# Differential attention with its outputs kept by tokens

## The chip, the cores and the metric

The kernel runs on one core of one Trainium2 chip. The metric is the time on the device in microseconds (us): the median of the runs shown. The engines are TensorE (PE, with its weight loads PEld), VectorE (DVE), ScalarE (ACT), GpSimd (POOL) and the DMA queues.

## The reference

The program is a stack of four token mixers and six feed-forward blocks on 512 tokens of 1024 features, all in float32. Only one part is touched: the second half of the first mixer, differential attention with 8 heads. `q`, `k` and `v` are projections of the normed input; each head has two queries and two keys of 64 features and one value of 128.

```python
def block(start, q1b, q2b):
    mask = chunk_causal_mask(start, s)
    p1 = masked_softmax(einsum('bqhd,bkhd->bhqk', q1b, k1) * scale, mask)
    p2 = masked_softmax(einsum('bqhd,bkhd->bhqk', q2b, k2) * scale, mask)
    return einsum('bhqk,bkhe->bqhe', p1 - lam * p2, vf)

o = sweep_query_blocks(block, q[:, :, :, 0], q[:, :, :, 1])
o = rms_norm(o, subln) * (1.0 - lam_init)      # over a head's 128 features
```

The result, 1024 features, goes through an output projection. What matters here is the last line: each token's 128 outputs of a head are divided by the root of their mean square, and multiplied by a gain per feature.

## The kernel before, in words

Every engine has its program, written out in a fixed order, and semaphores order them among each other. `mm` (L316) issues one matmul; `pe_three` (L319 to L321) issues the three products of a float32 projection split into a high and a low part. Weights come as units of 128 x 1024 into a ring of six: DMA fills RAW, ACT rounds it (`hi_to`, L301), DVE takes the rest (`lo_to`, L307), and PE reports with `unit_done` when it has used it.

The stage is `ev_attn` (L1055). Its PE program interleaves several things. For head h, `scores(h, step)` makes the products of queries and keys, in three steps, into PSUM banks 2 to 5; DVE takes their maxima (`maxes`), ACT the exponentials with their sums (`exps`), and DVE subtracts the second map from the first (`combined`). `turn(h, g)` transposes the result in ten blocks of 128 x 128 into bank 6, in three groups, and ACT copies each group to PT (`turned`). `values(h)` multiplies by the values into bank 7: the stationary operand is V, so the output has features on partitions and tokens along the row; four products of 512, 384, 256 and 128 columns. Meanwhile PE projects the queries and keys of the head two further on (`pieces` into banks 0 and 1); ACT copies them (`query`), PE rotates them (`rot`), DVE finishes the rotation (`rope`). For h = 0 to 4 that is the loop over `early(h)`, some 20 us an iteration; behind it the order is written out by hand, with pieces of the output projection (`out_tile(m, k0, k1)`, which needs `yl` of heads below k1) put among the attention of heads 5 to 7.

The norm of a head, before: ACT copies the outputs from bank 7 to O (three buffers) and squares them to OSQ (`out`). PE sums the squares over the partitions with four products of one column (`squares`, L1171), DVE adds epsilon (`mean_square`), two heads' roots are taken at once (`roots`, eleven small instructions of 0.17 us), DVE writes them on the diagonals of four blocks (`diagonal`, L1532), and PE multiplies a matrix of ones by these, which puts each token's scale in bank 7 on all partitions (`scales`, L1177). DVE multiplies O by it and by the gain (`scaled`, L1540), ACT rounds the product to YH (`rounded`, L1394), DVE writes the rest to YL (`low`, L1544) and counts `yl`. Bank 7 is thus shared by values, squares and scales. A wait of one engine on another is a `wait_ge` on the semaphore, in the order of the program.

Of the kernel before, what the change touches and what calls it, by code (L numbers as in the profile page):

```python
# [1054 lines left out]
def ev_attn(nc, b):  # L1055
# [32 lines left out]
    DGA = sb("da_dg", [P, T], at=WORK2 + 13 * KB)  # L1088
# [3 lines left out]
    DG = [DGA, DGA, DGA, AB, DGA, AB, DGA, AB]  # L1092
    s = {n: sem("da_" + n) for n in """in v_ready qs_ready rot_ready rope_done angle_ready trig_ready lam_e
         scores max_ready p_ready comb tr pt_ready o_ready osq ssq ss_taken dg bc scaled yh yl""".split()}
# [12 lines left out]
    GROUPS = {4: (0, 1)}  # L1107
# [7 lines left out]
    def pe(pe, e):  # L1115
# [45 lines left out]
        def values(h):  # L1161
            pe.wait_ge(s["pt_ready"], 3 * h + 3)
            if h:
                pe.wait_ge(s["ss_taken"], h)
            if h in (3, 5, 7):
                pe.wait_ge(s["scaled"], {3: 2, 5: 4, 7: 5}[h])
            for j in range(TT):
                last = mm(ps[:, 7, j * P:T], V[:, j, tile(h)], PT[:, PTO[j]:PTO[j] + (4 - j) * P], j == 0, j == 3)
            last.then_inc(s["o_ready"], 1)

        def squares(h):  # L1171
            pe.wait_ge(s["osq"], 2 * h + 2)
            for j in range(TT):
                last = mm(ps[:, 7, j:j + 1], OSQ[:, tile(j)], ones[:, 0:1])
            last.then_inc(s["ssq"], 1)

        def scales(h, after):  # L1177

            pe.wait_ge(s["dg"], h + 1)
            pe.wait_ge(s["ss_taken"], after + 1)  # L1180
            if h:
                pe.wait_ge(s["scaled"], h)
            mm(ps[:, 7, :], ones[:], DG[h][:]).then_inc(s["bc"], 1)

# [22 lines left out]
        def early(h):  # L1207
# [10 lines left out]
            if h >= 2:  # L1218
                squares(h - 2)
# [4 lines left out]
            if h == 4:  # L1224
                scales(0, h - 2)
# [5 lines left out]
            if h == 4:  # L1231
                scales(1, h - 2)
# [15 lines left out]
        squares(3)  # L1248
# [15 lines left out]
        squares(4)  # L1264
# [4 lines left out]
        scales(2, 4)  # L1269
# [5 lines left out]
        scales(3, 4)  # L1275
# [11 lines left out]
        squares(5)  # L1287
# [12 lines left out]
        squares(6)  # L1300
# [3 lines left out]
        scales(4, 6)  # L1304
# [6 lines left out]
        squares(NH - 1)  # L1311
        out_tile(3, 2, 4)
        scales(5, NH - 1)
# [3 lines left out]
        scales(6, NH - 1)  # L1317
        out_tile(5, 3, 5)
        out_tile(0, 5, 6)
        scales(7, NH - 1)  # L1320
# [4 lines left out]
        pe.wait_ge(s["scaled"], NH)  # L1325
        out_whole(pe, no + 6, SCAN_BANK[6])

    def act(act, own, e):
# [56 lines left out]
        def out(h):  # L1385
            act.wait_ge(s["o_ready"], h + 1)
            if h >= 3:
                act.wait_ge(s["yl"], h - 2)
            A(O[:, h % 3, :], ps[:, 7, :], ACT.Copy).then_inc(s["osq"], 1)
            if h:  # L1390
                act.wait_ge(s["ssq"], h)
            A(OSQ[:], ps[:, 7, :], ACT.Square).then_inc(s["osq"], 1)

        def rounded(h):  # L1394
            act.wait_ge(s["scaled"], h + 1)
            A(YH[:, h, :], O[:, h % 3, :], ACT.Copy).then_inc(s["yh"], 1)

        for h in range(5):
            gq, gk = 4 + 2 * h, 5 + 2 * h
            if h >= 1:  # L1400
                exps(h - 1, 2)
            query(gq)
            hi_to(act, unit_of(e, gq) + 5)
            if h >= 1:
                turned(h - 1, 0)
            exps(h, 0)
            exps(h, 1)
            if h >= 1:
                turned(h - 1, 1)
                turned(h - 1, 2)  # L1410
            query(gk)
            hi_to(act, unit_of(e, gk) + 5)
            for a in GROUPS.get(h, ()):
                rounded(a)
            if h >= 1:
                out(h - 1)
# [40 lines left out]
    def dve(dve, own, e, finish, tail):  # L1457
# [65 lines left out]
        def mean_square(h):  # L1523
            dve.wait_ge(s["ssq"], h + 1)
            eps = EP[:, 4 * (h % 2):4 * (h % 2) + 4]
            own(v.scalar_tensor_tensor(SS[:, 4 * h:4 * h + 4], ps[:, 7, 0:4], 1.0 / P, eps, ALU.mult, ALU.add), "ss_taken")
# [5 lines left out]
        def diagonal(h):  # L1532
            if h in (1, 2):
                dve.wait_ge(s["bc"], h)
            elif h >= 4:
                dve.wait_ge(s["bc"], h - 1)
            own(v.tensor_tensor(DG[h][:].rearrange("p (j n) -> p j n", n=P), ident[:, None, :].to_broadcast([P, TT, P]),
                                RS[:, 4 * h:4 * h + 4][:, :, None].to_broadcast([P, TT, P]), ALU.mult), "dg")

        def scaled(h):  # L1540
            dve.wait_ge(s["bc"], h + 1)
            own(v.scalar_tensor_tensor(O[:, h % 3, :], O[:, h % 3, :], GAIN[:], ps[:, 7, :], ALU.mult, ALU.mult), "scaled")

        def low(h):  # L1544
            dve.wait_ge(s["yh"], h + 1)
            own(v.tensor_tensor(YL[:, h, :], O[:, h % 3, :], YH[:, h, :].bitcast(F32), ALU.subtract), "yl")

        for h in range(5):
# [10 lines left out]
            rope(gq)  # L1559
            if h == 4:  # L1560
                scaled(0)
                diagonal(1)
                scaled(1)
            combined(h, (0, 1))
            lo_to(dve, unit_of(e, gk) + 5)
            if h == 4:
                low(0)
                low(1)
            if h == 3:
                roots((0, 1))  # L1570
                diagonal(0)
# [15 lines left out]
        diagonal(2)  # L1587
# [4 lines left out]
        scaled(2)  # L1592
        diagonal(3)
        maxes(7, 0)
        scaled(3)
        maxes(7, 1)
        combined(6, (2,))
        low(2)
# [6 lines left out]
        roots((4, 5))  # L1605
        mean_square(6)
        diagonal(4)
        lo_to(dve, no + 6)
        scaled(4)
        low(4)  # L1610
        diagonal(5)
        mean_square(7)
        roots((6, 7))
        scaled(5)
        diagonal(6)
        low(5)
        diagonal(7)
        scaled(6)
        low(6)
        scaled(7)  # L1620
# [2279 lines left out]
```

## Time and profile before

| | us |
|---|---|
| median of 3 runs | 3405.75 |
| lowest, highest | 3405.64, 3407.36 |
| span of the profiled execution | 3408.6 |
| PE busy in it | 3352.6 |
| attention stage, within the window 100 to 275 us: PE busy | 171.5 of 175 |
| the same: DVE, ACT busy | 123.7, 82.5 |
| the same: granted clock | 1.00 |

The profile has no time of its own for that execution beside its span; the span is 2.85 us above the median of the runs. A timeline row is: start, duration, engine and line, operation, output and inputs, how many were merged, and in brackets how long the engine stood idle before it and for whom. Durations of PE contain the time that a result needs to leave the array, so what a group costs is read from one start to the next or from the chain. A float32 product of `mm` shows as two instructions. Rows of `mm` all have line 316 and are told apart by their tiles: `da_pt,da_v` is values, `ones,da_osq` squares, `da_dg,ones` or `da_ab,ones` scales, `da_k,da_q` scores, and `ident,da_p` on line 1157 a turn.

### The profile page before, as it was taken

The page shows a single profiled execution, that of the slowest core. Times are in us where ns is not written, and L with a number is a line of the kernel's source. Part 1 is how long each engine was busy: PE and PEld are TensorE (multiplying, and loading weights), DVE is VectorE, ACT ScalarE, POOL GpSimd, SP SyncE. Part 2 cuts the span into 40 slices and gives each one's busy share as a digit, 9 for nine tenths or more (in the row PEclk, how much of TensorE's full clock was granted, in tenths as well). Part 3 has the DMA queues.
Part 4 walks back from the last instruction along what each step waited for, and adds up shares of the span by engine and source line. Part 5 has one row for each costly group of instructions (what it writes and reads, how often), then busy time and mean ns, then how long its engine had stood idle before and what let it go on. Part 6 is the DMA issues. An engine that isn't in the chain of part 4 may idle for free.

```text
span 3408.6 us, 42717 instructions
## 1 busy us (share of the span) xinstructions
PE 3352.6 (98%) x17244; PEld 2790.3 (82%) x17244; DVE 1832.8 (54%) x2984; ACT 1311.8 (38%) x2216; POOL 17.2 (1%) x53
## 2 busy tenths in 40 slices
PE   8999999999999999999999999999999999999998
PEld 7768888888878888898888778888888888788887
DVE  5676884433886543354436357443454336664446
ACT  4453443222575322242224355322342226653333
POOL 0000000000100000000000000000000000000000
PEclk9999999999999999999999999999999999999999
DMA  3103213223301222322232211322322232023244
GB/s 131 62 25 108 69 63 109 95 100 100 102 21 56 93 99 98 106 93 99 96 103 94 87 38 66 106 95 100 104 93 94 98 105 77 32 81 105 97 144 167
DMA packets 92568, 307.81 MB, mean 90 GB/s; under 512 B 16014, under 2 KB 17684, under 8 KB 92372
## 3 DMA queue, kind: packets, MB, share of 16 engines
q1 hardware_dynamic: 89528, 301.31, 26.4%
q10 hardware_dynamic: 2844, 3.77, 0.3%
q8 instruction: 137, 2.24, 0.3%
q14 instruction: 59, 0.48, 0.0%
HBM read 302.95 MB, written 2.10 MB: 89 GB/s over the span
## 4 chain that ended last, share of the span: by engine, by line
PE 90%; DVE 6%; ACT 3%; issue 1%; DMA 0%; SPq 0%; DVEq 0%; ACTq 0%
PE ps L319 25%; PE ps L321 25%; PE ps L320 25%; PE ps L316 14%; DVE WL L307 1%; ACT WH L301 1%; DVE R L709 1%; PE ps L3103 0%; DVE XL L884 0%; DVE XT L875 0%; DMA RAW<-units 0%; DVE XT L878 0%; ACT XH L646 0%; ACT R L644 0%; DVE S L722 0%
## 5 line engine op out<-in xcount | busy, mean ns | idle before, releaser
L319 PE MATMUL ps<-XH,WH 128*128 128x512 f32 (+1 forms) x3200 | 1188.0, 371 | 19.1 <-DVE XL L884 12.7
L321 PE MATMUL ps<-XH,WL 128*128 128x512 f32 (+1 forms) x3200 | 1171.0, 366 | 0.0
L320 PE MATMUL ps<-XL,WH 128*128 128x512 f32 (+1 forms) x3200 | 1170.4, 366 | 0.0
L307 DVE TENSOR_TENSOR WL<-RAW,WH 128x1024 fp32r<-128x1024 f32 x567 | 686.3, 1224 | 312.6 <-ACT WH L301 308.6
L319 PEld LDWEIGHTS ps<-XH,WH 128*128 128x128 f32 x3200 | 606.5, 190 | 125.6 <-DVE XL L884 11.4
L321 PEld LDWEIGHTS ps<-XH,WL 128*128 128x128 f32 x3200 | 606.4, 190 | 96.6
L320 PEld LDWEIGHTS ps<-XL,WH 128*128 128x128 f32 x3200 | 607.0, 190 | 95.9 <-issue 1.9
L301 ACT ACTIVATE WH<-RAW 128x1024 fp32r<-128x1024 f32 x567 | 587.3, 1050 | 150.3 <-DMA RAW<-units 91.4
L319 PE MATMUL ps<-HH,WH 128*128 128x512 f32 (+1 forms) x990 | 362.7, 366 | 0.0
L320 PE MATMUL ps<-HL,WH 128*128 128x512 f32 (+1 forms) x990 | 361.8, 365 | 0.0
L321 PE MATMUL ps<-HH,WL 128*128 128x512 f32 (+1 forms) x990 | 361.7, 365 | 0.0
L596 ACT ACTIVATE HH<-HV 128x512 fp32r<-128x512 f32 x132 | 83.4, 632 | 564.3 <-DVE HV L788 564.3
L788 DVE SCALAR_TENSOR_TENSOR HV<-SG,ps 128x512 f32<-128x512 f32 x132 | 90.7, 687 | 294.7 <-PE ps L321 294.3
L785 DVE SCALAR_TENSOR_TENSOR SG<-TH,ps 128x512 f32<-128x512 f32 x132 | 90.7, 687 | 290.2 <-ACT TH L593 290.0
L503 ACT ACTIVATE SQ<-R 128x512 f32<-128x512 f32 (+1 forms) x89 | 48.9, 550 | 483.9 <-DVE R L709 408.0
L709 DVE SCALAR_TENSOR_TENSOR R<-R,ps 128x512 f32<-128x512 f32 (+1 forms) x86 | 51.5, 599 | 336.6 <-PE ps L321 335.8
L593 ACT ACTIVATE TH<-ps 128x512 f32<-128x512 f32 x132 | 78.7, 596 | 360.6 <-PE ps L321 360.6
L319 PEld LDWEIGHTS ps<-HH,WH 128*128 128x128 f32 x990 | 186.7, 189 | 30.5
L321 PEld LDWEIGHTS ps<-HH,WL 128*128 128x128 f32 x990 | 186.7, 189 | 30.1
L320 PEld LDWEIGHTS ps<-HL,WH 128*128 128x128 f32 x990 | 186.7, 189 | 30.0
L790 DVE TENSOR_TENSOR HL<-HV,HH 128x512 fp32r<-128x512 f32 x132 | 91.4, 693 | 101.4 <-ACT HH L596 101.4
L646 ACT ACTIVATE XH<-XT,VEC 128x256 fp32r<-128x256 f32 x144 | 78.9, 550 | 32.8 <-DVE XT L875 32.7
(603 smaller groups left out, 3258.8 us busy)
## 6 DMA issues: line engine op xcount, KB each, us to landing
RAW<-units SPq DMA_DIRECT2D x567, 512.0 KB, 3.3
XIN<-in_x ACTq DMA_DIRECT2D x2, 1024.0 KB, 6.3
out<-YT SPq DMA_DIRECT2D x8, 256.0 KB, 3.2
mb_pairf<-constants ACTq DMA_DIRECT2D x1, 512.0 KB
GB<-in_ln_g SPq DMA_DIRECT2D x1, 512.0 KB
GB<-in_ln_b SPq DMA_DIRECT2D x1, 512.0 KB
da_pi<-in_positions ACTq DMA_DIRECT2D x1, 256.0 KB, 3.0
wa_dist<-constants ACTq DMA_DIRECT2D x1, 192.0 KB, 2.3
```

What stands on the lines that cost most here:

```text
L301: nc.scalar.activation(WH[:, u % RING, :], RAW[:, u % RING, :], ACT.Copy).then_inc(S["wh_ready"], 1)
L307: nc.vector.tensor_tensor(WL[:, u % RING, :], RAW[:, u % RING, :], WH[:, u % RING, :].bitcast(F32), ALU.subtract)\
L316: return nc.tensor.matmul(out, lhsT, rhs, start=start, stop=stop, **kw)
L319: nc.tensor.matmul(out, wh, xh, start=start, stop=False)
L320: nc.tensor.matmul(out, wh, xl, start=False, stop=False)
L321: return nc.tensor.matmul(out, wl, xh, start=False, stop=stop)
L596: nc.scalar.activation(HH[:, j, :], HV[:, j % 2, :], ACT.Copy).then_inc(S["ffn_act"], 1)
L646: nc.scalar.activation(XH[:, k, hs], XT[:, t % 4, :], ACT.Identity, scale=g, bias=b).then_inc(S["xh_ready"], 1)
L709: own(v.scalar_tensor_tensor(rk, rk, alpha, src, ALU.mult, ALU.add), "r_ready")
L785: own(v.scalar_tensor_tensor(SG[:, j % 2, :], TH[:, j % 2, :], 1.0, ps[:, b, :], ALU.add, ALU.mult))
L788: own(v.scalar_tensor_tensor(HV[:, j % 2, :], SG[:, j % 2, :], e["half"], ps[:, b + 1, :], ALU.mult, ALU.mult), "ffn_dve")
L790: own(v.tensor_tensor(HL[:, j, :], HV[:, j % 2, :], HH[:, j, :].bitcast(F32), ALU.subtract), "ffn_dve")
```

## The change

`values(h)` swaps its operands: the transposed map is stationary and V moves, in ten products of 128 columns, so the output in bank 7 has tokens on partitions. The sum over a head's features is then along the row: ACT squares with an accumulator, one instruction for each of four token tiles, straight to SS. `squares`, `diagonal` and `scales` are gone. DVE multiplies O by the roots row by row (`scaled`), PE transposes the product back in four blocks into bank 7 or, for heads 4 and 6, bank 3 (`back`), ACT rounds it from there with the gain as its scale, and DVE writes the rest, again from PSUM. The semaphores change with it: `values` waits for `ssq` instead of `ss_taken`, and for heads 3 and 5 for `yl` of 2 and 4; `back` waits for `scaled`, for `ssq` and for an earlier `yl`. The orders of DVE and ACT around them change as shown (context cut).

```diff
@@ -1085,13 +1085,12 @@
     PT = sb("da_pt", [P, 1280], at=WORK2 + 8 * KB)
-    DGA = sb("da_dg", [P, T], at=WORK2 + 13 * KB)
     AB = sb("da_ab", [P, T], at=WORK2 + 16 * KB)
...
-    DG = [DGA, DGA, DGA, AB, DGA, AB, DGA, AB]
+    BACK = (7, 7, 7, 7, 3, 7, 3, 7)
     s = {n: sem("da_" + n) for n in """in v_ready qs_ready rot_ready rope_done angle_ready trig_ready lam_e
-         scores max_ready p_ready comb tr pt_ready o_ready osq ssq ss_taken dg bc scaled yh yl""".split()}
+         scores max_ready p_ready comb tr pt_ready o_ready ssq scaled back yh yl""".split()}
     MX, NM, L, RC, N2 = sm[:, 0:8], sm[:, 8:24], sm[:, 24:40], sm[:, 40:48], sm[:, 48:52]
...
@@ -1104,7 +1103,6 @@
     PTO = (0, 512, 1024, 896)
-    GROUPS = {4: (0, 1)}
...
@@ -1161,26 +1159,24 @@
             if h:
-                pe.wait_ge(s["ss_taken"], h)
-            if h in (3, 5, 7):
-                pe.wait_ge(s["scaled"], {3: 2, 5: 4, 7: 5}[h])
-            for j in range(TT):
-                last = mm(ps[:, 7, j * P:T], V[:, j, tile(h)], PT[:, PTO[j]:PTO[j] + (4 - j) * P], j == 0, j == 3)
+                pe.wait_ge(s["ssq"], h)
+            if h in (3, 5):
+                pe.wait_ge(s["yl"], {3: 2, 5: 4}[h])
+            for i in range(TT):
+                for j in range(i + 1):
+                    last = mm(ps[:, 7, tile(i)], PT[:, PTO[j] + (i - j) * P:PTO[j] + (i - j + 1) * P], V[:, j, tile(h)], j == 0, j == i)
             last.then_inc(s["o_ready"], 1)
-        def squares(h):
-            pe.wait_ge(s["osq"], 2 * h + 2)
-            for j in range(TT):
-                last = mm(ps[:, 7, j:j + 1], OSQ[:, tile(j)], ones[:, 0:1])
-            last.then_inc(s["ssq"], 1)
-
-        def scales(h, after):
-
-            pe.wait_ge(s["dg"], h + 1)
-            pe.wait_ge(s["ss_taken"], after + 1)
-            if h:
-                pe.wait_ge(s["scaled"], h)
-            mm(ps[:, 7, :], ones[:], DG[h][:]).then_inc(s["bc"], 1)
+        def back(h, after):
+
+            pe.wait_ge(s["scaled"], h + 1)
+            if BACK[h] == 7:
+                pe.wait_ge(s["ssq"], after + 1)
+            if BACK.index(BACK[h]) < h:
+                pe.wait_ge(s["yl"], h if h < 4 else h - 1)
+            for i in range(TT):
+                last = nc.tensor.transpose(ps[:, BACK[h], tile(i)], O[:, h % 3, tile(i)], ident[:])
+            last.then_inc(s["back"], 1)
...
@@ -1215,21 +1211,19 @@
                 turn(h - 1, 0)
-            if h >= 2:
-                squares(h - 2)
             if h:
...
             if h == 4:
-                scales(0, h - 2)
+                back(0, h - 2)
             if h >= 1:
...
             if h == 4:
-                scales(1, h - 2)
+                back(1, h - 2)
             pieces(n2 + 2 * h + 1, ps[:, 1, :], XH, XL, 6, KD)
...
@@ -1245,7 +1239,6 @@
         pieces(n2 + 11, ps[:, 1, :], XH, XL, 0, 1)
-        squares(3)
         pieces(n2 + 11, ps[:, 1, :], XH, XL, 1, 3)
...
@@ -1261,18 +1254,17 @@
         scores(6, 2)
-        squares(4)
         turn(5, 1)
...
         out_tile(0, 0, 2)
-        scales(2, 4)
+        back(2, 4)
         scores(7, 0)
...
         scores(7, 1)
-        scales(3, 4)
+        back(3, 4)
         out_tile(1, 1, 2)
...
@@ -1284,7 +1276,6 @@
         out_tile(2, 1, 2)
-        squares(5)
         turn(6, 2)
...
@@ -1297,32 +1288,29 @@
         turn(7, 1)
-        squares(6)
         out_tile(3, 1, 2)
...
         turn(7, 2)
-        scales(4, 6)
+        back(4, 6)
         out_tile(4, 2, 3)
...
         out_tile(4, 3, 4)
-        squares(NH - 1)
+        back(5, NH - 1)
         out_tile(3, 2, 4)
-        scales(5, NH - 1)
         out_tile(4, 4, 5)
...
         out_tile(3, 4, 5)
-        scales(6, NH - 1)
+        back(6, NH - 1)
         out_tile(5, 3, 5)
         out_tile(0, 5, 6)
-        scales(7, NH - 1)
+        back(7, NH - 1)
         for m in range(1, 6):
...
             out_tile(m, 6, KD)
-        pe.wait_ge(s["scaled"], NH)
         out_whole(pe, no + 6, SCAN_BANK[6])
...
@@ -1385,15 +1373,17 @@
             if h >= 3:
-                act.wait_ge(s["yl"], h - 2)
-            A(O[:, h % 3, :], ps[:, 7, :], ACT.Copy).then_inc(s["osq"], 1)
+                act.wait_ge(s["back"], h - 2)
+            A(O[:, h % 3, :], ps[:, 7, :], ACT.Copy)
             if h:
                 act.wait_ge(s["ssq"], h)
-            A(OSQ[:], ps[:, 7, :], ACT.Square).then_inc(s["osq"], 1)
+            for i in range(TT):
+                last = A(OSQ[:, tile(i)], ps[:, 7, tile(i)], ACT.Square, accum_out=SS[:, 4 * h + i:4 * h + i + 1])
+            last.then_inc(s["ssq"], 1)
         def rounded(h):
-            act.wait_ge(s["scaled"], h + 1)
-            A(YH[:, h, :], O[:, h % 3, :], ACT.Copy).then_inc(s["yh"], 1)
+            act.wait_ge(s["back"], h + 1)
+            A(YH[:, h, :], ps[:, BACK[h], :], ACT.Copy, scale=GAIN[:]).then_inc(s["yh"], 1)
...
@@ -1405,13 +1395,15 @@
             exps(h, 1)
+            if h == 4:
+                rounded(0)
             if h >= 1:
...
                 turned(h - 1, 2)
+            if h == 4:
+                rounded(1)
             query(gk)
             hi_to(act, unit_of(e, gk) + 5)
-            for a in GROUPS.get(h, ()):
-                rounded(a)
             if h >= 1:
...
@@ -1523,27 +1515,19 @@
             eps = EP[:, 4 * (h % 2):4 * (h % 2) + 4]
-            own(v.scalar_tensor_tensor(SS[:, 4 * h:4 * h + 4], ps[:, 7, 0:4], 1.0 / P, eps, ALU.mult, ALU.add), "ss_taken")
+            own(v.scalar_tensor_tensor(SS[:, 4 * h:4 * h + 4], SS[:, 4 * h:4 * h + 4], 1.0 / P, eps, ALU.mult, ALU.add))
...
-        def diagonal(h):
-            if h in (1, 2):
-                dve.wait_ge(s["bc"], h)
-            elif h >= 4:
-                dve.wait_ge(s["bc"], h - 1)
-            own(v.tensor_tensor(DG[h][:].rearrange("p (j n) -> p j n", n=P), ident[:, None, :].to_broadcast([P, TT, P]),
-                                RS[:, 4 * h:4 * h + 4][:, :, None].to_broadcast([P, TT, P]), ALU.mult), "dg")
-
         def scaled(h):
-            dve.wait_ge(s["bc"], h + 1)
-            own(v.scalar_tensor_tensor(O[:, h % 3, :], O[:, h % 3, :], GAIN[:], ps[:, 7, :], ALU.mult, ALU.mult), "scaled")
+            o = O[:, h % 3, :].rearrange("p (j n) -> p j n", n=P)
+            own(v.tensor_tensor(o, o, RS[:, 4 * h:4 * h + 4][:, :, None].to_broadcast([P, TT, P]), ALU.mult), "scaled")
...
             dve.wait_ge(s["yh"], h + 1)
-            own(v.tensor_tensor(YL[:, h, :], O[:, h % 3, :], YH[:, h, :].bitcast(F32), ALU.subtract), "yl")
+            own(v.scalar_tensor_tensor(YL[:, h, :], ps[:, BACK[h], :], GAIN[:], YH[:, h, :].bitcast(F32), ALU.mult, ALU.subtract), "yl")
...
@@ -1557,18 +1541,16 @@
             rope(gq)
+            combined(h, (0, 1))
             if h == 4:
-                scaled(0)
-                diagonal(1)
-                scaled(1)
-            combined(h, (0, 1))
+                low(0)
             lo_to(dve, unit_of(e, gk) + 5)
             if h == 4:
-                low(0)
                 low(1)
...
                 roots((0, 1))
-                diagonal(0)
+                scaled(0)
+                scaled(1)
...
@@ -1584,18 +1566,16 @@
         maxes(6, 1)
-        diagonal(2)
+        scaled(2)
         mean_square(4)
...
         rope(15)
-        scaled(2)
-        diagonal(3)
+        scaled(3)
         maxes(7, 0)
-        scaled(3)
+        low(2)
         maxes(7, 1)
         combined(6, (2,))
-        low(2)
         low(3)
...
@@ -1603,21 +1583,17 @@
         roots((4, 5))
+        scaled(4)
         mean_square(6)
-        diagonal(4)
+        scaled(5)
         lo_to(dve, no + 6)
-        scaled(4)
         low(4)
-        diagonal(5)
         mean_square(7)
         roots((6, 7))
-        scaled(5)
-        diagonal(6)
+        scaled(6)
+        scaled(7)
         low(5)
-        diagonal(7)
-        scaled(6)
         low(6)
-        scaled(7)
         low(7)
...
```

## Rows read from the trace of the kernel before

**Rows 1.** The page: busy time of each engine; the chain that ended last, by engine.
```profile
PE 3352.6 (98%) x17244; PEld 2790.3 (82%) x17244; DVE 1832.8 (54%) x2984; ACT 1311.8 (38%) x2216; POOL 17.2 (1%) x53
...
PE 90%; DVE 6%; ACT 3%; issue 1%; DMA 0%; SPq 0%; DVEq 0%; ACTq 0%
```

**Rows 2.** Chain of waits, 110 to 275 us: start us, us on the chain, what.
```profile
241.01 0.44 PE ps L1157 x4
...
248.25 2.39 PE ps L316 x8
...
254.08 0.79 PE ps L316 x8
254.87 0.35 PE ps L319
255.21 0.23 PE ps L320
...
256.38 0.86 PE ps L316 x2
```

**Rows 3.** Timeline of PE in the stage behind: start us, us, instructions [idle before].
```profile
322.45 1.05 PE L316 MATMUL ps<-mb_bc 128*128 128x128 f32 x8
323.33 0.49 PE L1696 MATMUL ps<-ident,mb_bc 128*128 128x128 f32 x3
```

**Rows 4.** Timeline of PE in the attention stage.
```profile
165.07 0.38 PE L1157 MATMUL ps<-ident,da_p 128*128 128x128 f32 x2
...
189.57 2.42 PE L316 MATMUL ps<-da_pt,da_v 128*128 128x512 f32 x8
...
216.94 1.05 PE L316 MATMUL ps<-ones,da_osq 128*128 128x1 f32 x8 [0.99 <-ACT da_osq L1392]
...
223.35 1.13 PE L316 MATMUL ps<-da_k,da_q 64*128 64x512 f32 x4 [1.75 <-DVE da_k L1480]
...
228.84 2.39 PE L316 MATMUL ps<-da_pt,da_v 128*128 128x512 f32 x8 [0.30 <-DVE da_o L1542]
...
248.25 2.39 PE L316 MATMUL ps<-da_pt,da_v 128*128 128x512 f32 x8 [0.23 <-DVE da_o L1542]
```

**Rows 5.** Groups of instructions by shape, 100 to 275 us.
```profile
L316 PEld LDWEIGHTS ps<-da_pt,da_v 128*128 128x128 f32 x64 | 11.6, 189 | 8.4 <-issue 5.2
```

**Rows 6.** Timeline of ACT in the attention stage.
```profile
123.58 0.37 ACT L1375 ACTIVATE da_p<-ps,da_small 128x128 f32<-128x128 f32 x1
...
123.92 0.38 ACT L1375 ACTIVATE da_p<-ps,da_small 128x128 f32<-128x128 f32 x1
...
163.89 0.60 ACT L1383 ACTIVATE da_pt<-ps 128x512 f32<-128x512 f32 x1
...
189.50 1.05 ACT L301 ACTIVATE WH<-RAW 128x1024 fp32r<-128x1024 f32 x1
...
215.81 0.59 ACT L1389 ACTIVATE da_o<-ps 128x512 f32<-128x512 f32 x1
...
216.77 0.59 ACT L1375 ACTIVATE da_p<-ps,da_small 128x384 f32<-128x384 f32 x1
...
235.05 0.60 ACT L1383 ACTIVATE da_pt<-ps 128x512 f32<-128x512 f32 x1 [0.95 <-PE ps L1157]
```

**Rows 7.** Timeline of DVE in the attention stage.
```profile
184.95 0.75 DVE L1542 SCALAR_TENSOR_TENSOR da_o<-da_o,da_gain,ps 128x512 f32<-128x512 f32 x1
...
188.50 0.17 DVE L1511 RECIPROCAL da_small<-da_small 128x3 f32<-128x3 f32 x1
...
190.66 1.23 DVE L307 TENSOR_TENSOR WL<-RAW,WH 128x1024 fp32r<-128x1024 f32 x1
...
219.23 0.18 DVE L1511 RECIPROCAL da_small<-da_small 128x3 f32<-128x3 f32 x1
```

**Rows 8.** Timeline of PE near 496 us, in a later stage.
```profile
495.77 0.39 PE L319 MATMUL ps<-XH,WH 128*128 128x256 f32 x1 [2.64 <-DVE XL L887]
```

**Rows 9.** Windows: us, busy per engine, granted clock (PEclk), DMA share, GB/s.
```profile
496.00:500.00 4.00, 4.00 (x21) 3.82 (x21) 3.63 (x8) 2.37 (x4) 0.00 (x0) 0.59 0.02 4
```

## The prediction

> **What bounds the kernel now.** I read the page first: TensorE (PE) is busy 98% of the span, DVE 54%, ACT 38%, and PE carries 90% of the chain that ended last [rows 1]. So work taken off PE counts in full wherever PE doesn't then wait, and a new wait of PE counts in full as well; DVE or ACT time counts only through such a wait. The PE timeline of the attention stage then gives the order of work, and four places where PE does wait: 0.99 us ahead of the squares of head 4, 1.75 ahead of the first scores of head 7, 0.30 and 0.23 ahead of the values of heads 5 and 7 [rows 4]. All that is edited lies between 127 and 265 us.
>
> **PE's work, per head.** The chain prices a PE group by what it adds to the path [rows 2]. Squares: eight pieces 0.79 us, and the matmul behind them takes 0.35 instead of 0.23, so 0.91. The broadcast of scales (two passes over 512 columns): 0.86. Both go. Four transposes come: the same form costs 0.44. Values: now 8 instructions (each product takes two passes), 2560 columns in all, 2.39 us of path; after, 20 instructions of 128 columns, the same columns. The trace has that form: 8 of 128x128 take 322.45 to 323.33, 0.11 each, so 20 take 2.20 [rows 3], and with the 0.12 that the next matmul loses 2.32. From -0.07 to a weight load that stops overlapping (20 by 189 ns, 3.8 us, +1.4 [rows 5]) I take no difference, by the row of the same form. PE is thus rid of 0.91 + 0.86 - 0.44 = 1.33 per head, 10.6 in all, and 0.99 + 0.30 + 0.23 of waits ahead of squares 4 and values 5 and 7 could go: 12.1 us if nothing else came late.
>
> The Trainium skill, "TensorE: Matmul & The Clock Gate", section LDWEIGHTS, puts a load of 128 columns at 128/1.2 = 107 ns whatever the rows. Added to the pass instead of hidden, twelve more loads would be 1.3 us a head and 10 us in all by that figure; the 0.11 per load and matmul together says that they overlap.
>
> **ACT and DVE.** ACT's one square of 512 (copy and square 215.81 to 216.77, 0.48 each) becomes four of 128 with an accumulator read each; exps of that width with their read come every 0.34 (123.58 to 123.92) [rows 6]. So 1.36, 0.9 more per head, between the output copy and what ACT does next. Bounds: 0.3 apiece if the missing bias pointer saves a little, 0.6 apiece if the 0.37 of the one and its read did not overlap with the next. DVE loses the diagonals (0.69) and writes the same 0.69 for the row scaling; `low` reads PSUM, 0.75 like the multiplication at 184.95 [rows 7]. mean_square no longer waits for PE. None of this matters except where a wait of PE hangs on it, so I walk PE's waits; times are those of before, shifts are noted.
>
> **Heads 2 and 3 of the loop (130 to 170 us): -0.5 each, not -0.9.** With squares gone PE reaches the last turn 0.91 sooner, 164.16 instead of 165.07. It needs ACT's copy of the turn before, 163.89 + 0.60 = 164.49, which hangs on exps that no edit moves. So it starts at 164.55 [rows 4, 6]: 0.52 gained, 0.4 turned into a wait. Twice: -1.05.
>
> **Head 4 (170 to 192 us): +3.3.** Three edits meet. (1) `back(1)` writes bank 7, so it waits for `low(0)`, and DVE does that behind rope and combined. Rope ended at 184.95 and PE's rotation that it waited for comes 0.9 sooner, of which some 0.6 is felt: 184.3. Combined with its upkeep took 188.50 to 190.66: 186.45. low(0) 0.75: 187.2. PE's turn ahead of it ends near 185.3, a stall of about 1.9; the broadcast it replaces began at 186.48 and cost twice as much, so PE leaves 0.2 later than before. (2) `values(3)` now waits for two `yl`, and `low(1)` sits on DVE behind lo_to, which waits for ACT's rounding of a weight, which ACT does behind query, which waits for PE to end the projection just before. Before: ACT rounds at 189.50, DVE's split starts at 190.66. With +0.2 the split starts at 190.85, is left 1.15 later, low(1) 192.0 to 192.75, values at 192.9 instead of 189.57 [rows 4, 6, 7]. PE has only scores(4,2) to do meanwhile: a stall of 3.1. Queued behind it are rot(13) and the next projection; ACT and DVE behind them wait for PE and lie inside the shift. This is the largest term. Sum so far +2.25.
>
> **Heads 5 to 7.** squares(3) gives -0.91. squares(4) and its wait of 0.99 vanish, but scores(7,0) waits for rope(15), the end of a DVE run that waits for exps(6,1). ACT's output copy goes from 215.81 to 214.90, squares end 0.49 + 1.36 later, 216.75, where exps(6,1) used to start: no gain. DVE's combined goes from 219.23 to 218.85, since it had followed a max that waited for PE. scores(7,0) goes from 223.35 to 222.97. So of 0.91 + 0.91 + 0.99 + 0.42 only 0.4 arrives; PE idles from 218.2, some 4.7 us. Then low(2) needs rounded(2), behind PE's turn(5,2): 225.4; low(2) ends 226.4; back(3) at 226.55, about even with the broadcast at 226.7. values(5) needs low(3): maxes(7,1) end with their scaling at 228.1, combined (a max's scaling, five small ones and a product, about 1.25) at 229.35, low(3) 230.1, values at 230.25 instead of 228.84: +1.4, a stall of 2.5. Then squares(5) gives 0.91 but ACT's 0.9 longer output delays its copy of turn(6,1) from 235.05 to 236.5, so the next turn goes from +1.4 to +0.8 only. squares(6) -0.91, broadcast 4 -0.42, wait ahead of values(7) -0.23: -0.75. Last, squares(7) and three exchanges: -0.91 - 3 x 0.42, so -2.9 at the end; low(6) and low(7) are needed 4 us after they are done. With +2.25: -0.65 us, where PE's own work fell by 10.6.
>
> **The clock.** Ahead of 495.77 PE was idle for 2.64 us, and the next 4 us had a granted clock of 0.59: 4 x 0.41 = 1.64 us lost, the lower of the two levels (1.2 against 2.4 GHz) for most of it [rows 8, 9]. Four new stalls (1.9, 3.1, 4.7, 2.5 us) can each call it; the idle 1.75 ahead of the scores of head 7 did not (the stage had full clock throughout). Behind values(3) PE works without a wait and would pay in full. I take one such fall: +1.65. The Trainium skill ("TensorE: Matmul & The Clock Gate", Part 1) says "the default state is throttled, and activity releases the throttle"; the row above agrees.
>
> Sum: -0.65 + 1.65 = +1.0 on the profiled span, 3408.6 to 3409.6. That execution's span is 2.85 above the median of the runs, 3405.75; the difference carries over, so 3406.8.
>
> **Rivals.** A. *The stalls are not there*, because the lows or ACT come earlier than I walk: the 12.1 us above, 3393.7. For: DVE is half idle. Against: the order of each engine's work is fixed, and low(1) stands behind a weight that waits for PE. Halfway, with the values(3) stall gone only: 3403. B. *No fall of the clock*: -0.65, 3405.1. C. *A fall behind each of the four stalls*: -0.65 + 4 x 1.64 = +5.9, 3411.7; from one more stall of 1 us on it is measurably slower. D. *Weight loads bound the values*: 20 x 0.189 = 3.8 instead of 2.39, +1.4 a head and +11 in all, 3405.75 - 0.65 + 11 = 3416, slower; it decides from 0.17 us per instruction (1.0 more a head). For: da_pt's loads show 189 ns. Against: 0.11 for the pair.
>
> **Chances.** One or two falls, 3405.5 to 3409: 0.50. B 0.20. Halfway 0.10. A 0.08. C 0.08. D 0.04. What can be told from no change here is 0.2%, 6.8 us. Faster than that: A and a little of halfway, 0.10. Slower: D and half of C, 0.08. Within: 0.82. The range 3400 to 3411 leaves out A, D and most of C.
>
> **What would show it.** Waits of PE: on DVE `da_yl` ahead of values(3), about 3 us, and of values(5), about 2.5; on ACT `da_pt` ahead of the last turn of heads 2 and 3, 0.4 each; on DVE rope ahead of scores(7,0), over 4. Values at 0.11 per instruction; four squares within 1.4 us; a granted clock under 1.00 between 190 and 235 us. PE's busy time should fall by about 9 and its idle rise as much. I am wrong if PE passes values(3) without a wait, or if values take over 2.6 us.

## Result and profile after

The changed kernel takes 3413.15 us (median of 20 runs, 3406.88 to 3416.84). The kernel before, run beside it, takes 3407.66 (20 runs, 3404.12 to 3411.68; the three runs known ahead had 3405.75). The ratio is 1.0013, interval 1.0007 to 1.0019: 4.4 us slower, 2.4 to 6.5. (The two medians lie 5.5 us apart, the means of the same runs, 3412.41 and 3407.95, 4.5.) The prediction was 3406.8, so a slowdown of 1.0, and a range that ended at 3411: too low, and the range missed. The profiled execution of the changed kernel took 3413.99, its span 3412.0.

The page of the kernel after, busy time and chain by engine, beside [rows 1]:

```profile
PE 3346.2 (98%) x17292; PEld 2792.6 (82%) x17292; DVE 1827.3 (54%) x2976; ACT 1315.1 (39%) x2272; POOL 17.6 (1%) x53
...
PE 89%; DVE 7%; ACT 3%; issue 1%; DMA 0%; DVEq 0%; ACTq 0%
```

PE has 6.4 us less busy time and the kernel is longer, so PE must stand idle where it did not before. The timeline of PE between 127 and 255 us says where (start us, us, what, idle before it and for whom):

```profile
127.59 2.50 PE L316 MATMUL ps<-da_v,da_pt 128*128 128x128 f32 x20
129.92 1.02 PE L316 MATMUL ps<-da_qs,da_perm 128*128 128x512 f32 x2
...
164.22 0.44 PE L1155 MATMUL ps<-ident,da_p 128*128 128x128 f32 x2
...
184.35 0.44 PE L1155 MATMUL ps<-ident,da_p 128*128 128x128 f32 x2 [0.23 <-ACT da_pt L1371]
...
186.49 0.63 PE L1178 MATMUL ps<-ident,da_o 128*128 128x128 f32 x4 [1.70 <-DVE da_yl L1530]
...
192.22 4.10 PE L316 MATMUL ps<-da_v,da_pt 128*128 128x128 f32 x20 [3.05 <-DVE da_yl L1530]
196.16 1.02 PE L316 MATMUL ps<-da_qs,da_perm 128*128 128x512 f32 x2
...
226.88 2.08 PE L316 MATMUL ps<-da_k,da_q 64*128 64x512 f32 x4 [4.18 <-DVE da_k L1472]
...
235.63 3.31 PE L316 MATMUL ps<-da_v,da_pt 128*128 128x128 f32 x20 [2.48 <-DVE da_yl L1530]
...
254.38 2.39 PE L316 MATMUL ps<-da_v,da_pt 128*128 128x128 f32 x20
```

The waits of 0.99, 1.75, 0.30 and 0.23 of [rows 4] have become 1.70, 3.05, 4.18 and 2.48: 11.4 us of idle where there were 3.3. None of the four is for anything that the change computes anew. Two values and one exchange back wait until `low` has read bank 7 (`da_yl`), and the scores of head 7 wait for rope as before, longer.

Three of the four stalls are followed by a stretch at a lower clock. Windows of the kernel after (us, busy time of PE, PEld, DVE, ACT, POOL, granted clock, DMA share, GB/s):

```profile
192.00:196.00 4.00, 3.78 (x19) 3.81 (x20) 1.63 (x4) 0.00 (x0) 0.00 (x0) 0.58 0.02 4
192.22:198.00 5.78, 5.78 (x27) 5.12 (x28) 2.19 (x5) 1.64 (x10) 0.00 (x0) 0.70 0.01 3
226.88:232.00 5.12, 5.12 (x25) 3.11 (x26) 2.85 (x5) 2.33 (x4) 0.00 (x0) 0.67 0.00 0
235.63:241.00 5.37, 5.37 (x32) 4.74 (x33) 1.85 (x5) 0.06 (x1) 0.00 (x0) 0.68 0.00 0
```

The first is read as in [rows 9]: 4 us at 0.58. The other three begin where PE starts again and reach past the end of the fall, so that idle time isn't counted: 5.78 x 0.30 + 5.12 x 0.33 + 5.37 x 0.32 = 1.7 + 1.7 + 1.7 = 5.1 us of clock lost. The values of head 3 show it: 20 instructions take 3.94 from start to start (192.22 to 196.16) against 2.33 at full clock (127.59 to 129.92). That is the lower of the two levels, 1.2 GHz, for most of the stretch. The four windows of 20 us from 186 to 266 all show 1.00 in the kernel before; two of them:

```profile
206.00:226.00 20.00, 17.26 (x98) 11.09 (x96) 16.97 (x35) 11.38 (x38) 0.00 (x0) 1.00 0.08 27
226.00:246.00 20.00, 19.70 (x109) 15.07 (x106) 13.02 (x41) 11.47 (x28) 0.00 (x0) 1.00 0.00 1
```

To compare kernels closer than whole runs allow, I use one stretch of PE: from values(0) to the next stage's first group of `mb_bc`. The first row and the group of the kernel before (the group's line: line, tiles, count, banks, first start to last end):

```profile
127.35 2.42 PE L316 MATMUL ps<-da_pt,da_v 128*128 128x512 f32 x8
L316 PE MATMUL ps<-mb_bc x16: 270/275/275, 322.4 to 329.9; 128*128 128x128 f32 x16
```

and the group of the kernel after:

```profile
L316 PE MATMUL ps<-mb_bc x8: 270/275/275, 326.5 to 327.3; 128*128 128x128 f32 x8
```

The stage went from 195.10 (127.35 to 322.45, [rows 3]) to 198.90 us (127.59 to 326.49), +3.8, which lies within the ratio's 2.4 to 6.5. The spans of the two profiled executions differ by 3.4 (3412.0 and 3408.6), so the rest of the program adds nothing in these two: the loss lies here.

### The profile page after: what moved, and what is told of

It is laid out like the page before. It is cut to its first block, busy times and chain, and to the rows that moved or that the text cites. A ratio compares the mean times of both kernels' runs of the same rounds, so it can differ in the third digit from the quotient of the medians.

```text
span 3412.0 us, 42845 instructions
## 1 busy us (share of the span) xinstructions
PE 3346.2 (98%) x17292; PEld 2792.6 (82%) x17292; DVE 1827.3 (54%) x2976; ACT 1315.1 (39%) x2272; POOL 17.6 (1%) x53
## 3 DMA queue, kind: packets, MB, share of 16 engines
q8 instruction: 138, 2.26, 0.3%
## 4 chain that ended last, share of the span: by engine, by line
PE 89%; DVE 7%; ACT 3%; issue 1%; DMA 0%; DVEq 0%; ACTq 0%
PE ps L319 25%; PE ps L320 24%; PE ps L321 24%; PE ps L316 14%; DVE WL L307 1%; ACT WH L301 1%; DVE R L709 1%; DVE XL L884 0%; DVE XT L875 0%; PE ps L3079 0%; DVE XT L878 0%; ACT XH L646 0%; DVE da_small L1490 0%; ACT R L644 0%; DMA RAW<-units 0%
## 5 line engine op out<-in xcount | busy, mean ns | idle before, releaser
L319 PE MATMUL ps<-XH,WH 128*128 128x512 f32 (+1 forms) x3200 | 1188.5, 371 | 18.2 <-DVE XL L884 12.1
L319 PEld LDWEIGHTS ps<-XH,WH 128*128 128x128 f32 x3200 | 607.1, 190 | 124.6 <-DVE XL L884 11.4
```

The costliest lines, as they stand in the source:

```text
L319: nc.tensor.matmul(out, wh, xh, start=start, stop=False)
```

## Experiments

Two theories stood at the start. *Stalls and clock*: the order in which DVE and ACT do their work turned the saved PE work into four stalls, and the clock falls behind them make the rest of the loss. *PE's own work* (the rival): weight loads or the exchange back cost more than the walk gives them.

"Stage" in the table is the stretch just described, read from the one profiled execution of each kernel; the time and the ratio are those of whole runs.

| kernel | median us | ratio to before, interval | stage us |
|---|---|---|---|
| before | 3407.66 | 1 | 195.10 |
| after | 3413.15 | 1.0013, 1.0007 to 1.0019 | 198.90 |
| 1 fill | 3407.93 | 1.0000, 0.9991 to 1.0009 | 194.15 |
| 2 low(1) earlier | 3405.65 | 0.9994, 0.9985 to 1.0003 | 192.52 |
| 3 rope(15) earlier | 3409.98 | 1.0009, 1.0000 to 1.0018 | 198.17 |
| 4 before, rope(15) earlier | 3408.72 | 1.0000, 0.9991 to 1.0009 | 194.96 |
| after, again | 3411.75 | 1.0010, 1.0001 to 1.0019 | 198.53 |
| 5 all orders | 3398.22 | 0.9968, 0.9957 to 0.9979 | 187.12 |
| 6 and another bank | 3397.51 | 0.9965, 0.9953 to 0.9978 | 185.15 |
| 6 again | 3398.17 | 0.9966, 0.9952 to 0.9980 | 185.16 |
| 7 one square | 3418.26, one time | – | 199.91 |
| 8 best order | 3398.93 | 0.9971, 0.9959 to 0.9982 | 184.67 |

**1. Fill the stalls.** Products nobody reads, put into three of the four stalls, where PE would stand idle. The waits of the kernel after stay; one more, on `p_ready`, stands ahead of the four products, which write a bank that ACT must have read.

```diff
@@ values(h), ahead of the wait on ssq
+            if h in (3, 5):
+                for _ in range({3: 3, 5: 2}[h]):
+                    mm(ps[:, 6, :], ident[:], COS[:])
@@ ahead of scores(7, 0)
+        pe.wait_ge(s["p_ready"], 8 * 6 + EXPS[1])
+        for _ in range(4):
+            mm(ps[:, 4, :], ident[:], COS[:])
```

> The changed kernel with extra float32 matmuls (identity by the cosines, 0.86 us each, into a PSUM bank that is free then) ahead of three of PE's new waits: three ahead of values(3), four ahead of scores(7,0), two ahead of values(5). They are shorter than the stalls they stand in (3.05, 4.18, 2.48 us). Theory 'clock' (the term I mis-sized): the stalls' ends stay where they are, the three falls of the granted clock between 190 and 240 us are gone, and with them 1.6 us each: about 4.5 us less than the changed kernel, so a ratio to the kernel before of 0.9995 to 1.0005. Rival 'the falls cost nothing, the stalls are the whole loss': the same time as the changed kernel, ratio 1.0013.

Timeline of PE and windows of this kernel:

```profile
188.92 2.84 PE L316 MATMUL ps<-da_cos,ident 128*128 128x512 f32 x6
192.04 2.47 PE L316 MATMUL ps<-da_v,da_pt 128*128 128x128 f32 x20 [0.28 <-DVE da_yl L1536]
194.34 1.02 PE L316 MATMUL ps<-da_qs,da_perm 128*128 128x512 f32 x2
...
225.05 1.13 PE L316 MATMUL ps<-da_k,da_q 64*128 64x512 f32 x4 [0.47 <-DVE da_k L1478]
```

```profile
190.00:200.00 10.00, 9.72 (x49) 7.13 (x48) 7.49 (x14) 4.44 (x15) 0.00 (x0) 1.00 0.09 33
225.00:240.00 15.00, 14.22 (x85) 10.21 (x86) 9.76 (x22) 8.73 (x29) 0.00 (x0) 1.00 0.00 0
```

values(3) starts as late as before the fill (64.64 us after values(0), against 64.63) but now takes 2.30, and both windows shown have the full clock. The stage is 4.75 us shorter, close to the 5.1 that the three windows of the kernel after lost. Whole runs bear it out: all 11 of this kernel took 3409.05 or less, and of the 31 of the kernel after (the 20 above, 11 in its repeat below) only four did. The stage is also 0.95 shorter than in the kernel before, near the walk's 0.65 without any fall. So the loss splits: without the falls the stage would be no longer than in the kernel before, and the falls are more than the 3.8 us by which it is. (Trainium skill, "TensorE: Matmul & The Clock Gate", Part 1: it is activity that releases the throttle; this run agrees, since work without any use keeps the clock.)

**2. low(1) ahead of the weight.** On DVE, the instruction that frees bank 7 no longer stands behind a split that waits for ACT.

```diff
                 low(0)
+                low(1)
             lo_to(dve, unit_of(e, gk) + 5)
-            if h == 4:
-                low(1)
```

> The changed kernel with low(1) ahead of the weight split on DVE in head 4, nothing else. Theory 'order of DVE': the stall of 3.05 us ahead of values(3) goes nearly whole (low(1) ends near 188.5, values(3) starts within 0.3 us of scores(4,2)), the fall of the clock behind it goes too: 3.0 + 1.6 = 4.6 us less than the changed kernel, ratio to before near 1.000. Rival 'the weight is needed first' (the split delayed by low(1) delays the projection behind): less than 2 us gained. The waits in heads 6 and 7 stay as they are in all theories.

The stall ahead of values(3) is gone without a rest; the others stay at 1.71, 4.17 and 2.50. Windows of this kernel:

```profile
188.00:200.00 12.00, 12.00 (x72) 9.24 (x72) 9.08 (x16) 6.58 (x18) 0.00 (x0) 1.00 0.25 86
221.79:227.00 5.21, 5.21 (x26) 3.21 (x27) 2.95 (x5) 3.23 (x7) 0.00 (x0) 0.67 0.00 0
230.00:234.00 4.00, 3.46 (x30) 3.21 (x31) 2.33 (x6) 0.33 (x2) 0.00 (x0) 1.00 0.00 0
```

I expected 4.6 us, and the stage is 6.4 shorter: 3.05 of stall, 1.7 of the fall behind it, and 1.7 because the fall behind the stall of values(5) did not come either, with a stall there as long as in the kernel after. So the place where low(1) stands cost 4.7 us, and a stall of 2.5 us has a fall behind it in some executions and in others not. In whole runs too the interval of this kernel (0.9985 to 1.0003) lies clear of that of the kernel after (1.0007 to 1.0019). That the order on DVE makes the stall ahead of values(3) is shown.

**3 and 4. rope(15) ahead of the combination of head 6**, in the kernel after and in the kernel before.

```diff
-        combined(6, (0, 1))
         rope(15)
+        combined(6, (0, 1))
```

> The changed kernel with rope(15) ahead of combined(6, (0, 1)) on DVE, so that it no longer stands behind exps(6,1), which stands behind the four squares of head 4 on ACT. Theory: rope(15) starts at 222.05 instead of 224.8, scores(7,0) starts 2.7 us sooner, the wait falls from 4.18 to about 1.5, and the clock's fall behind it may go (another 1 to 1.6 us); values(5) gains what scores(7,1) gains, 2 to 2.7. In all 2.5 to 4.5 us less than the changed kernel. Rival 'ACT is the bound there': exps(7,0) and low(3) end no sooner, and under 1 us arrives at values(6).

> The kernel before with the same move of rope(15) alone, as a control: its wait of 1.75 us ahead of scores(7,0) should go, and 1 to 1.75 us of time, ratio 0.9995 to 0.9997. If it gains as much as the same move in the changed kernel, the long stall there isn't the doing of the change.

Timeline of PE of the kernel after with the move, and two of its windows:

```profile
225.04 1.13 PE L316 MATMUL ps<-da_k,da_q 64*128 64x512 f32 x4 [1.45 <-DVE da_k L1472]
...
230.15 0.63 PE L1178 MATMUL ps<-ident,da_o 128*128 128x128 f32 x4 [1.68 <-DVE da_yl L1530]
...
233.70 4.61 PE L316 MATMUL ps<-da_v,da_pt 128*128 128x128 f32 x20 [2.23 <-DVE da_yl L1530]
```

```profile
191.89:198.00 6.11, 6.11 (x23) 5.13 (x24) 1.44 (x3) 1.46 (x9) 0.00 (x0) 0.51 0.01 3
233.70:240.00 6.30, 6.30 (x32) 5.80 (x33) 1.84 (x5) 0.12 (x1) 0.00 (x0) 0.59 0.00 0
```

I expected 2.5 to 4.5 us, and the stage got 0.7 shorter. The wait for rope fell from 4.18 to 1.45 as meant, but 1.68 came up ahead of the exchange back(3), because low(2) stands on DVE behind combined(6, (0, 1)), scaled(3) and maxes(7, 0) and starts only at 229.25. Together with values(5) that is 5.36 us of idle for 6.66. The falls were two, but longer: 6.11 x 0.49 + 6.30 x 0.41 = 5.6 us lost for 5.1. -1.3 + 0.5 = -0.8, where the stage shows -0.7. In the kernel before, the same move took away the whole wait of 1.75 and gave 0.14 us, where I expected 1 to 1.75; a window of that kernel:

```profile
216.81:223.00 6.19, 6.19 (x22) 3.95 (x22) 4.58 (x11) 3.27 (x13) 0.00 (x0) 0.72 0.00 0
```

Behind the squares' wait of 0.99, that window of the kernel before with the move lost 6.19 x 0.28 = 1.7 us, where the kernel before without it had the full clock. So a fall took what the wait gave back; that the move caused the fall, one profile can't show. Without the clock the move is worth 0.14 + 1.7 = 1.9 us in the kernel before, and 1.3 us of idle in the kernel after. So rope(15) stood badly before the change too; what the change added is the length of the wait, 4.18 for 1.75. The move alone is no remedy, for either kernel.

**5. All orders at once**: low(1) and rope(15) as above, and

```diff
@@ DVE
         scaled(3)
+        low(2)
         maxes(7, 0)
-        low(2)
+        low(3)
         maxes(7, 1)
         combined(6, (2,))
-        low(3)
@@ ACT
-        exps(7, 0)
         rounded(3)
+        exps(7, 0)
```

> The changed kernel with three orders mended: low(1) ahead of the weight split, rope(15) ahead of combined(6, (0, 1)), and for heads 2 and 3 low(2) ahead of maxes(7,0), low(3) ahead of maxes(7,1), rounded(3) ahead of exps(7,0). Theory: the stalls were orders of DVE and ACT, so waits ahead of values(3) 0, scores(7,0) 1.5, values(5) at most 1; the wait of 1.7 ahead of back(1) stays. From values(0) to the next stage 195.1 us before, 198.9 with the change: here 190 to 191 us, total 4 to 5 us under before, ratio 0.9986. Rival: exps(7,1) comes later by the two lows, and the loss goes to turn(6,1): 192 or more.

PE waits 1.70, 1.44, 0.23 and 1.03, and the window of 186 to 226 us has a granted clock of 1.00:

```profile
186.00:226.00 40.00, 37.06 (x224) 27.39 (x225) 32.09 (x71) 24.50 (x74) 0.00 (x0) 1.00 0.12 41
```

The stage is 187.12, below the 190 to 191 that I expected and 11.8 us shorter than in the kernel after: idle is 4.4 for 11.4, 7.0 less, and the 5.1 of the falls makes 12.1. The kernel, PE's work being that of the change exactly, is 0.32% *faster* than the kernel before (0.21 to 0.43%).

**6. Another bank for the exchange of head 1.** back(1) writes bank 0, which is free until the next projection, and so need not wait for low(0).

```diff
-    BACK = (7, 7, 7, 7, 3, 7, 3, 7)
+    BACK = (7, 0, 7, 7, 3, 7, 3, 7)
@@ back(h, after)
+            if h == 1:
+                pe.wait_ge(s["rope_done"], 13)
@@ values(h)
-                pe.wait_ge(s["yl"], {3: 2, 5: 4}[h])
+                pe.wait_ge(s["yl"], {3: 1, 5: 4}[h])
@@ ahead of the projection of rotation 14
+        pe.wait_ge(s["yl"], 2)
```

> As e5_all, and head 1 is transposed back into bank 0 (free once rope(12) has read it) instead of bank 7, so back(1) doesn't wait for low(0), values(3) waits for low(0) alone, and the projection into bank 0 waits for low(1). Theory: the last new wait of head 4, 1.7 us, goes and nothing takes its place: 1.7 us less than e5_all, 188.5 to 189.5 from values(0) to the next stage, 6 to 7 us under before, ratio 0.998. Rival: PE then waits as long for ACT's or DVE's part of the same head (rounded(1) behind turned(3,2), low(1) behind combined): no gain over e5_all.

> e6_bank0 again beside e8_best, on the same chip: waits of PE 1.44, 0.2 and 1.0 us in heads 6 and 7 and none of 3 us, no fall of the clock in the stage, ratio to before 0.996 to 0.998.

All waits of over 0.2 us that the timeline of PE shows between 186 and 270 us:

```profile
217.21 1.13 PE L316 MATMUL ps<-da_k,da_q 64*128 64x512 f32 x4 [1.44 <-DVE da_k L1475]
...
220.86 0.63 PE L1180 MATMUL ps<-ident,da_o 128*128 128x128 f32 x4 [0.21 <-DVE da_yl L1533]
...
223.22 2.47 PE L316 MATMUL ps<-da_v,da_pt 128*128 128x128 f32 x20 [1.03 <-DVE da_yl L1533]
```

and its window:

```profile
186.00:226.00 40.00, 37.31 (x234) 27.71 (x232) 33.62 (x77) 25.18 (x78) 0.00 (x0) 1.00 0.12 41
```

The 1.70 is gone and the stage 2.0 shorter than in 5 (185.15; 185.16 in the repeat), where I expected 1.7; the 188.5 to 189.5 had been counted from the 190 to 191 expected of 5. Against the kernel after, the sum closes: idle goes from 11.4 to 2.7, 8.7 less, and with the 5.1 of the falls that is 13.8, where 13.75 are measured. In whole runs 5 and 6 can't be told apart. The repeat gave 0.9966 against 0.9965. Against the kernel before the stage is 9.95 us shorter; the ratios say 12 (7 to 16). The gain is real, and its size about 10.

**The kernel after once more**, beside 5 and 6 on the same chip, to see what repeats.

> The changed kernel again, on the same chip as the mended ones. The stalls (1.7, 3.05, 4.2, 2.5 us) should repeat to within 0.1; the falls of the clock in the stage should be three or more again if idle stretches call them, though not at the same instants. Ratio 1.001 to 1.002.

```profile
191.81 4.61 PE L316 MATMUL ps<-da_v,da_pt 128*128 128x128 f32 x20 [3.06 <-DVE da_yl L1530]
```

```profile
191.81:198.00 6.19, 6.19 (x24) 5.30 (x25) 1.51 (x4) 1.55 (x10) 0.00 (x0) 0.54 0.01 3
227.60:233.00 5.40, 5.40 (x28) 3.29 (x29) 3.13 (x5) 3.22 (x7) 0.00 (x0) 0.68 0.01 3
236.00:240.00 4.00, 3.65 (x31) 3.40 (x32) 2.14 (x6) 0.14 (x2) 0.00 (x0) 1.00 0.00 0
```

The waits repeat to 0.02 us: 1.70, 3.06, 4.18, 2.50. The falls do not: one long (6.19 x 0.46 = 2.85 us lost), one short (5.40 x 0.32 = 1.7), none behind the stall of values(5). I had expected three or more. That is 4.6 us lost for 5.1, and the stage is 0.4 shorter.

**7. One square instead of four.** The kernel after, but ACT squares 512 columns with one accumulator instead of four times 128. So the sums of squares per token are not formed (their tile is filled with ones), and the kernel leaves out the right scales.

> The changed kernel with ACT's four squares of 128 columns put back to one of 512 with a single accumulator (the sums per token are not formed, so the norms are left out of the result). It prices the four: by the trace 1.00 us for four with their reads against 0.6 for one with its read, so exps(6,1) starts 0.4 us sooner and scores(7,0) with it; the wait ahead of it 3.8 instead of 4.18; nothing else moves. If the accumulator reads were the cause of the long stall, it would be under 2.

Timeline of ACT in this kernel, and then in the kernel after:

```profile
220.86 0.60 ACT L1380 ACTIVATE da_osq<-ps 128x512 f32<-128x512 f32 x1
221.34 0.21 ACT L1380 ACTIVATION_READ_ACCUMULATOR da_osq<-ps 128x1 f32 x1
221.43 0.59 ACT L1363 ACTIVATE da_p<-ps,da_small 128x384 f32<-128x384 f32 x1
```

```profile
219.69 0.28 ACT L1381 ACTIVATE da_osq<-ps 128x128 f32<-128x128 f32 x1
219.84 0.21 ACT L1381 ACTIVATION_READ_ACCUMULATOR da_osq<-ps 128x1 f32 x1
219.94 0.29 ACT L1381 ACTIVATE da_osq<-ps 128x128 f32<-128x128 f32 x1
...
220.69 0.62 ACT L1363 ACTIVATE da_p<-ps,da_small 128x384 f32<-128x384 f32 x1
```

Four squares with their reads hold ACT 1.00 us (219.69 to 220.69), one holds it 0.57 (220.86 to 221.43). The 0.43 arrive at the scores of head 7 in full: they wait 3.72 instead of 4.18, where I had expected 3.8. The stage was 1.0 longer all the same, since this execution had four falls, one of them behind the stall of 1.70 at 186 us:

```profile
186.33:191.00 4.67, 4.22 (x16) 2.94 (x16) 0.00 (x0) 1.89 (x3) 0.00 (x0) 0.63 0.08 11
```

That is 4.67 x 0.37 = 1.7 us more lost, and 0.6 less idle in the four stalls: +1.1. One time of the whole, 3418.26, proves nothing beyond it.

**8. The best order I could find**, from 6, with rope(15) ahead of maxes(6, 2), the mean square behind it, maxes(7, 0) ahead of low(2), and combined(6, (0, 1)) between low(2) and low(3).

```diff
         scaled(2)
-        mean_square(4)
-        maxes(6, 2)
         rope(15)
-        combined(6, (0, 1))
+        maxes(6, 2)
+        mean_square(4)
         scaled(3)
-        low(2)
         maxes(7, 0)
+        low(2)
+        combined(6, (0, 1))
         low(3)
```

> As e6_bank0, with DVE's order in heads 6 and 7 turned further: rope(15) ahead of maxes(6,2), mean_square(4) behind it, scaled(3), maxes(7,0) and low(2) ahead of combined(6, (0, 1)), low(3) ahead of maxes(7,1). Theory: rope(15) ends at 215.6 instead of 217.2, so the wait of 1.44 ahead of scores(7,0) goes; back(3) then waits for low(2) about 0.5, values(5) starts about 1.0 sooner, at 222.2 instead of 223.2, and the stage is 1 us shorter than e6_bank0. Rival: exps(7,1) and combined(7, ...) come later by as much and turn(6,1) waits: no gain.

The scores of head 7 no longer wait. But back(3) waits 0.55 and values(5) 1.51, where 6 had 0.21 and 1.03, and the stage gains 0.5 of the 1 that I expected. In whole runs (0.9971) it can't be told from 6 (6 again, beside it: 0.9966).

## Why the prediction was wrong

It held wherever it walked the waits, and failed in the number of clock falls. The position of a piece in the kernel after, less that before and less the 0.24 by which values(0) started later, against the walk and the clock lost by then (windows above):

| piece | walk | clock lost | sum | measured |
|---|---|---|---|---|
| last turn, head 3 | -1.05 | 0 | -1.05 | -1.09 |
| values(3) | +2.25 | 0 | +2.25 | +2.41 |
| scores(7,0) | +1.85 | 1.7 | +3.55 | +3.29 |
| values(5) | +3.65 | 3.4 | +7.05 | +6.55 |
| values(7) | +1.50 | 5.1 | +6.6 | +5.89 |
| next stage | -0.65 | 5.1 | +4.45 | +3.80 |

- **PE's work.** Right. Values take 2.33 from start to start, 0.07 more than the 2.26 of before (127.35 to 129.61), where I took no difference; rival D, loads in the open, is out. The four transposes of an exchange take 0.44 (181.69 to 182.13) or less, squares and broadcasts are gone. In this trace too the `da_v,da_pt` loads show 192 ns each in the median, and hide. PE's busy time fell by 6.4 and not by the 9 of the prediction; the 5.1 us of lower clock are busy time too.
- **Heads 2 and 3.** Right, -1.09 for -1.05.
- **Head 4.** Right: 1.70 for the predicted 1.9, 3.05 for 3.1, each for the instruction named. Experiment 2 took away the larger by moving the `low` alone, 6 the other by the bank, with the waits that go with it: the two reasons are shown, not only argued.
- **Heads 5 to 7.** Right in kind. The scores of head 7 waited 4.18, not 4.7, one reason being the squares: 0.25 apiece, not the 0.34 that I took from exps of the width, and 1.00 for four instead of 1.36. values(5) waited 2.48 for 2.5.
- **The clock.** This is the step that failed, a term of the sum that was too small: 1.65 us for falls of the clock, where 5.1 were measured. "I take one such fall: +1.65." The price per fall was right (1.7 each), the number was three. -0.65 + 3 x 1.65 = +4.3 comes near the ratio's 4.4, in part by luck: without the falls the stage shows 3.80 - 5.1 = -1.3 and not -0.65. My only evidence for fewer falls was the stall of 1.75 that had none behind it; but three of the four stalls were longer than that, and the row nearest to them, 2.64 us with a fall of 0.59 [rows 8, 9], had one. I priced four stalls by the shortest. Rival C, a fall behind each, had the 3411.7 that was nearest to the truth, and a chance of 0.08 that was too small.
- **Range and base.** Three falls for one add 3.3 to the 3406.8 and give 3410.1, still in the range; the 0.65 by which the walk of the stage errs (4.45 against 3.80) is no matter either. What left the range was the clock together with the base: the median before moved from 3405.75 over three runs to 3407.66 over twenty, 1.9 more, and the last 1.1 is what the two medians lie further apart than the ratio says. The sum set the profiled span, 3408.6, against those three runs and let the 2.85 between them carry over. But each run on record with both figures has a time 1.9 to 2.5 us above its own span. So the profiled execution took some 3410.6 (an estimate from these), and the three runs of the base were low ones among 3404.12 to 3411.68. This spread goes with the granted clock: of the 33 runs of the kernel before beside experiments 1 to 4, the 11 with a mean clock of 0.995 have a mean time of 3410.3, the four with 0.998 one of 3404.0.

Where did the gain go, then? 10.6 us of PE's work were to be taken away. Values took about 0.5 of it back (0.07 a head, but nothing for head 7, where both kernels show 2.15 from start to start), the last turns of heads 2 to 4 about 0.25 each for ACT's copy (164.22, where 163.74 + 0.23 was due, with no wait shown by the timeline), 0.7; new idle took 8.1 (11.4 for 3.3), the clock 5.1. -10.6 + 0.5 + 0.7 + 8.1 + 5.1 = +3.8, which the stage shows. Experiment 6 gives most of it back without touching PE's work: with 2.7 of idle for 3.3 the same sum is -10.6 + 0.5 + 0.7 - 0.6 = -10.0, and the stage is 9.95 shorter than before. That its whole runs gain 12 us, the 12.1 of the prediction's case of no stalls, is chance within their interval.

What stays open is what decides whether a given stall has a fall behind it, and how long it is. Nearly the same four stalls had three falls, two (one of them long) and, in experiment 7, four. Nor does a fall start at a fixed place: in the repeat the clock fell at about 190.7, while PE still stood idle ahead of values(3), and again at about 228.2, 0.6 us after PE had ended the wait for rope. One execution of each kernel was profiled, so how often a stall of a given length has a fall rests on the few counts below.

## What to carry to other kernels

When work is taken off the engine that bounds a kernel, list the buffers it now waits for and where in the other engines' fixed order each is freed: here one `low` behind a weight split that waited for PE itself cost 3.05 us of stall and 1.7 of clock, more than three heads' saved work. Price a new stall of PE by what rows of its length show. In the profiled executions of this stage all eight stalls of 2.9 to 4.2 us had a fall of the clock behind them, three of five of 2.2 to 2.5 us, and two of nineteen of 1.0 to 1.75; a fall cost 1.7 us, in three cases 2.6 to 3.0. Orders are best repaired together: moving rope(15) alone gave 0.7 us and low(1) alone 6.4, all of them gave 11.8.

## What was unexpected of the hardware

- A PE stall is dearer than it is long. Behind idle of 3.05 us PE lost 1.7 us of clock; in another execution of the same program, behind the same 3.06 us, 2.85. A stall of 2.5 us had a fall behind it in the kernel after and in experiment 7, and none in the repeat and in experiment 2. Of the seven profiled executions in which no stall of the stage was longer than 1.75 us (the kernel before, experiments 1, 4, 5, 6 twice, 8) only that of experiment 4 had a fall there.
- Work without use is worth issuing in such a stall: nine float32 products of 512 columns, in a stage of 199 us, shortened it by 4.75 us, as they did not delay what came behind.
- A short wait can precede a fall: 0.72 over 6.19 us behind 0.99 us of idle (experiment 4), and 0.63 over 4.67 us behind 1.70 (experiment 7). The kernels before and after, with the same waits, had none there.
- An ACT square of 128 columns with an accumulator read repeats every 0.25 us (219.69, 219.94), an exp of the same width with a bias pointer every 0.34 [rows 6].
